# Eight gate tiles ahead of attention by four seven-product units, four plain units inside it

## The reference: a macaron layer with a gated mixer in its middle

```python
proj = u @ w_in                      # u is (1024, 1024), w_in is (1024, 4096)
# columns: xp 512 | q 512 | k 512 | v 512 | gate_logits 2048
y_pool = causal_pool_mixer(xp, pool_w_group, pool_scale) @ w_branch_pool
o_sb = stick_breaking_attention(q, k, v)      # 8 heads of 64, 128 query rows at a time
y_sb = o_sb @ w_branch_attn
g = sigmoid(gate_logits)
g_pool, g_sb = split(g, 2)                    # 8 tiles of 128 channels each
h = h + (g_pool * y_pool + g_sb * y_sb) @ w_out
```

## Time and profile before

| | |
|---|---|
| median of 3 runs | 1911.35 us (1911.08 to 1912.22) |
| the profiled execution | 1911.22 us, its span 1909.3 us |
| PE busy | 1899.8 us, 100% of the span, 8998 matmuls |
| DVE, ACT, POOL busy | 1370.5 us (72%), 799.4 us (42%), 135.0 us (7%) |
| granted PE clock | full in all 40 slices |
| DMA | 348.24 MB, 182 GB/s on average |

### The profile page before, as it was taken

One profiled execution on the slowest core, in us unless ns is written; L12 is line 12 of the kernel. 1 busy time (PEld: TensorE's weight loads), 2 busy tenths in 40 slices (PEclk: granted clock), 3 DMA queues, 4 the chain that ended last, 5 costly groups with the idle time before them and its releaser, 6 DMA issues.

```text
span 1909.3 us, 24938 instructions
## 1 busy us (share of the span) xinstructions
PE 1899.8 (100%) x8998; PEld 1591.0 (83%) x8998; DVE 1370.5 (72%) x1686; ACT 799.4 (42%) x1177; POOL 135.0 (7%) x157
## 2 busy tenths in 40 slices
PE   9999999999999999999999999999999999999998
PEld 9888888888888888888888888898888888888886
DVE  6977777784565786469677768889777777755655
ACT  7423232323434544324577762473323232334344
POOL 1000000000000200000145420010000000000001
PEclk9999999999999999999999999999999999999999
DMA  5456654558676733423866557634455445677665
GB/s 165 151 198 228 225 178 142 198 189 307 209 237 204 199 110 133 133 72 106 242 175 176 138 163 261 185 128 134 165 162 179 167 152 163 222 262 239 205 194 201
DMA packets 258419, 348.24 MB, mean 182 GB/s; under 512 B 29344, under 2 KB 161184, under 8 KB 255008
## 3 DMA queue, kind: packets, MB, share of 16 engines
q1 hardware_dynamic: 258016, 346.62, 56.2%
q10 hardware_dynamic: 320, 0.52, 0.1%
HBM read 233.83 MB, written 112.99 MB: 182 GB/s over the span
## 4 chain that ended last, share of the span: by engine, by line
PE 97%; DVE 1%; DMA 1%; ACT 0%; issue 0%; SPq 0%; POOL 0%; POOLq 0%; ACTq 0%
PE bank L1271 41%; PE bank L1327 8%; PE bank L1328 8%; PE bank L1329 8%; PE bank L1380 8%; PE bank L1520 7%; PE bank L1223 3%; PE bank L1430 2%; PE bank L1458 2%; PE bank L1488 2%; PE bank L1590 2%; PE bank L1609 1%; PE bank L1608 1%; PE bank L1198 1%; PE bank L1575 1%; PE bank L1573 1%
## 5 line engine op out<-in xcount | busy, mean ns | idle before, releaser
L2270 DVE TENSOR_TENSOR dn_lo<-dn_lo_raw,dn_hi 128x1024 fp32r<-128x1024 f32 x149 | 181.7, 1223 | 150.9 <-ACT dn_hi L1793 150.3
L1271 PE MATMUL bank<-hi_t,wa_lo 128*128 128x512 f32 x656 | 252.8, 389 | 0.0
L1271 PE MATMUL bank<-lo_t,wa_hi 128*128 128x512 f32 x656 | 252.8, 389 | 0.0
L1271 PE MATMUL bank<-hi_t,wa_hi 128*128 128x512 f32 x656 | 252.7, 389 | 0.0
L1793 ACT ACTIVATE dn_hi<-dn_lo_raw 128x1024 fp32r<-128x1024 f32 x149 | 157.9, 1061 | 220.2 <-DMA dn_lo_raw<-act_dram 220.2
L1327 PE MATMUL bank<-dn_hi 128*128 128x512 f32 x596 | 232.5, 390 | 0.0
L1329 PE MATMUL bank<-dn_lo,dn_hi 128*128 128x512 f32 x596 | 231.9, 389 | 0.0
L1328 PE MATMUL bank<-dn_hi,dn_lo 128*128 128x512 f32 x596 | 231.9, 389 | 0.0
L1271 PE MATMUL bank<-hi_b,wa_hi 128*128 128x512 f32 x492 | 190.4, 389 | 0.0
L1271 PE MATMUL bank<-lo_b,wa_hi 128*128 128x512 f32 x492 | 190.4, 389 | 0.0
L1271 PE MATMUL bank<-hi_b,wa_lo 128*128 128x512 f32 x492 | 190.4, 389 | 0.0
(11 more groups left out here) (275 smaller groups left out, 3846.0 us busy)
## 6 DMA issues: line engine op xcount, KB each, us to landing
wa_lo_raw<-in_ffn_w_gate_up_dram SPq DMA_DIRECT2D x87, 512.0 KB, 5.0
dn_lo_raw<-act_dram SPq DMA_DIRECT2D x149, 256.0 KB, 4.3
act_dram<-g SPq DMA_DIRECT2D x44, 512.0 KB, 4.4
wd_t<-in_ffn_w_down_dram SPq DMA_DIRECT2D x44, 512.0 KB, 6.7
act_dram<-s_of SPq DMA_DIRECT2D x88, 256.0 KB, 6.4
wd_dram<-wd_t SPq DMA_DIRECT2D x22, 1024.0 KB, 5.9
dn_lo_raw<-wd_dram SPq DMA_DIRECT2D x85, 256.0 KB, 3.3
dn_lo_raw<-in_ffn_w_down_dram SPq DMA_DIRECT2D x64, 256.0 KB, 3.0
```

The source lines that it names most:

```text
L1271: last = nc.tensor.matmul(acc, lhs, rhs, start=n == 0 and i != 2 and i < 5, stop=n == 11, skip_group_check=True)
L2270: return nc.vector.tensor_tensor(dst, raw, hi.bitcast(f32), ALU.subtract)
```

## The change

`EARLY` goes from 6 to 8. By the formulas this makes `MIX_UNITS` one gate unit longer (`NM` = 8: two of q and k, four of attention gates, two of `xp`), and `GATE_UNITS` one shorter (`NG` = 4: all eight kind 0 tiles in pairs, 16 banks, 384 matmuls). All eight attention gate tiles are then made by seven-product units. `U_C` falls from 13 to 12.

With eight units, the last of which must again end on the lower quad, unit 0 now takes the upper quad. So the second plain unit of q and k moves to banks 0 to 3, behind the first one, and waits for each bank to be emptied; the first seven-product unit waits for the last transpose instead of for banks, and the second one waits for the banks of the second plain unit. The ring buffers' places, counted from the end, turn by one. The rest of the diff restates parities: `b + NM + 1` becomes `b + 1`, `4 * m + b` becomes `b`, and the branch weights go to half `j % 2`.

```diff
-EARLY = 6
+EARLY = 8
 GATE_UNITS = tuple(((0, j), (0, j + 1)) for j in range(0, EARLY, 2)) + tuple(((0, j), (1, j)) for j in range(EARLY, KT))
...
                 for b in range(4):
                     th, ab = b // 2, b % 2
-                    if not fresh:
-                        pe.wait_ge(tr_free, 4 * NT)
+                    wait_bank(b, q)
...
-                        last = products(bank[:, b if fresh else 4 + b, :], par, ab, lambda kt: u_hi[:, kt, cols],
+                        last = products(bank[:, b, :], par, ab, lambda kt: u_hi[:, kt, cols],
...
             def mix_unit(b):
 
-                s = (b + NM + 1) % 2
+                s = (b + 1) % 2
                 for i in range(7):
                     place, hi, lo, (kind, slot) = PRODUCTS[i]
-                    if b < 2 and i in (0, 1, 3, 4):
-                        wait_bank(place, Q_A[b] + 1)
+                    if b == 0 and i == 0:
+                        pe.wait_ge(tr_free, 4 * NT)
+                    if b == 1 and i in (0, 1, 3, 4):
+                        wait_bank(place, Q_A[1] + 1)
...
             for j in range(KT):
-                branch_tile(j, (U_C + j) % 2, j // 2)
+                branch_tile(j, j % 2, j // 2)
...
-                nc.scalar.activation(ring_hi[n % 3][:, th * HALF:(th + 1) * HALF], bank[:, 4 * m + b, :], ACT.Copy,
+                nc.scalar.activation(ring_hi[n % 3][:, th * HALF:(th + 1) * HALF], bank[:, b, :], ACT.Copy,
...
-            act.wait_ge(raw_in[U_C % 2], 32 * (U_C // 2 + 1))
+            act.wait_ge(raw_in[KT % 2], 32 * (U_C // 2 + 1))
```

More of the change, by code:

```diff
@@ L1974, in mix_first @@
                 act.wait_ge(mb_prod, 7 * b + 1)
-                nc.scalar.activation(mix_dst(b, 0, 0), bank[:, 4 * ((b + NM + 1) % 2), :], ACT.Copy).then_inc(mb_copied, 1)
+                nc.scalar.activation(mix_dst(b, 0, 0), bank[:, 4 * ((b + 1) % 2), :], ACT.Copy).then_inc(mb_copied, 1)
             def mix_second(b):
@@ L1981, in mix_second @@
                     act.wait_ge(mb_add, 5 * b)
-                nc.scalar.activation(mid[:, :], bank[:, 4 * ((b + NM + 1) % 2), :], ACT.Copy).then_inc(mb_copied, 1)
+                nc.scalar.activation(mid[:, :], bank[:, 4 * ((b + 1) % 2), :], ACT.Copy).then_inc(mb_copied, 1)
             def mix_post(b, a, th, adds):
@@ L2238, in outputs_hi @@
                 nc.scalar.activation(o_piece(u_hi, i), o_piece(xu, i), ACT.Copy).then_inc(o_hi, 1)
-            act.wait_ge(raw_in[U_C % 2], 32 * (U_C // 2 + 1))
+            act.wait_ge(raw_in[KT % 2], 32 * (U_C // 2 + 1))
             act.wait_ge(gate_ready, GATE_LAST[NG - 2] + 1)
-            nc.scalar.activation(w_hi[:, U_C % 2, 0, 0:BR], w_raw[:, U_C % 2, 0, 0:BR], ACT.Copy).then_inc(whi, 1)
+            nc.scalar.activation(w_hi[:, KT % 2, 0, 0:BR], w_raw[:, KT % 2, 0, 0:BR], ACT.Copy).then_inc(whi, 1)
             for i in range(len(O_PARTS)):
@@ L2249, in split_branch @@
             def split_branch(j):
-                act.wait_ge(raw_in[(U_C + j) % 2], 32 * ((U_C + j) // 2 + 1))
+                act.wait_ge(raw_in[j % 2], 32 * ((U_C + j) // 2 + 1))
                 act.wait_ge(acc_ready, 4 * Q_C + 2 * (j - 1))
-                nc.scalar.activation(w_hi[:, (U_C + j) % 2, 0, 0:BR], w_raw[:, (U_C + j) % 2, 0, 0:BR], ACT.Copy).then_inc(whi, 1)
+                nc.scalar.activation(w_hi[:, j % 2, 0, 0:BR], w_raw[:, j % 2, 0, 0:BR], ACT.Copy).then_inc(whi, 1)
             for n in range(1, KT):
@@ L2719, in take_first @@
                 cols = slice(th * HALF, (th + 1) * HALF)
-                nc.vector.scalar_tensor_tensor(out=ring_lo[(2 * m + ab) % 3][:, cols], in0=bank[:, 4 * m + b, :], scalar=1.0 if ab else QSCALE,
+                nc.vector.scalar_tensor_tensor(out=ring_lo[(2 * m + ab) % 3][:, cols], in0=bank[:, b, :], scalar=1.0 if ab else QSCALE,
                                                in1=ring_hi[(2 * m + ab) % 3][:, cols].bitcast(f32), op0=ALU.mult,
@@ L2784, in mix_c11 @@
                 dst = mix_dst(b, 0, 0)
-                nc.vector.tensor_tensor(dst, bank[:, 4 * ((b + NM + 1) % 2) + 1, :], dst, ALU.add).then_inc(mb_add, 1)
+                nc.vector.tensor_tensor(dst, bank[:, 4 * ((b + 1) % 2) + 1, :], dst, ALU.add).then_inc(mb_add, 1)
             def mix_c22(b, part):
-                dst, s = mix_dst(b, 1, 1), (b + NM + 1) % 2
+                dst, s = mix_dst(b, 1, 1), (b + 1) % 2
                 if part:
@@ L2805, in mix_c12 @@
                 dve.wait_ge(mb_prod, 7 * b + 6)
-                nc.vector.tensor_tensor(mix_dst(b, 0, 1), bank[:, 4 * ((b + NM + 1) % 2) + 2, :], mid[:, :], ALU.add).then_inc(mb_add, 1)
+                nc.vector.tensor_tensor(mix_dst(b, 0, 1), bank[:, 4 * ((b + 1) % 2) + 2, :], mid[:, :], ALU.add).then_inc(mb_add, 1)
             def mix_c21(b):
                 dve.wait_ge(mb_prod, 7 * b + 7)
-                nc.vector.tensor_tensor(mix_dst(b, 1, 0), bank[:, 4 * ((b + NM + 1) % 2) + 3, :], mid[:, :], ALU.add).then_inc(mb_add, 1)
+                nc.vector.tensor_tensor(mix_dst(b, 1, 0), bank[:, 4 * ((b + 1) % 2) + 3, :], mid[:, :], ALU.add).then_inc(mb_add, 1)
             def mix_out(b, a, th, posts):
@@ L3145, in split_branch @@
                 dve.wait_ge(whi, U_C + j + 1)
-                dst, raw, hi = (flat(w[:, (U_C + j) % 2, 0, 0:BR]) for w in (w_lo, w_raw, w_hi))
+                dst, raw, hi = (flat(w[:, j % 2, 0, 0:BR]) for w in (w_lo, w_raw, w_hi))
                 nc.vector.tensor_tensor(dst, raw, hi.bitcast(f32), ALU.subtract).then_inc(wlo, 1)
```

4 lines of the change are left out of this document (2 added, 2 removed).

## The result

| | before | after |
|---|---|---|
| median | 1911.3 us (1911.08 to 1912.22) | 1921.45 us (1921.23 to 1923.36) |
| ratio, 95% interval | | 1.0055 (1.0044 to 1.0067) |
| profiled execution, span | 1911.2, 1909.3 us | 1922.66, 1920.7 us |
| PE matmuls | 8998 | 8986 |
| attention: first gate matmul to branch | 215.7 us | 208.6 us |

The prediction said 1912.8, range 1909.0 to 1916.0. The change is slower, and by twice as much as the worst case that I had priced, +4.7. The trace of after is of an execution 1.2 us above its median, so sums over the trace come out about 1 us above sums of medians.

A forecast was written before the change was run, and what follows sets the result against it. PE was taken to bound the kernel, busy 1899.8 of 1909.3 us. The terms +19.0 - 22.1 + 0.6 + 4.0 + 0.1 gave +1.6 us on 1911.22, so 1912.8 us, range 1909.0 to 1916.0.

The forecast's parts named there:

- the worst case that I had priced: Attention: the waits at the weighs at their upper bound of 7 us, making the change +4.7 us, 1915.9.
- Parts 1, 2, 3 and 5: Added seven-product unit +19.0 us; second plain unit in lower banks 0; 96 attention matmuls gone -22.1; end of attention +0.1.
- Part 4 (a): First logits of attention: PE arrives 0.7 us earlier and waits for the q load, +0.6 us, bounds 0 and 0.7.
- Part 4 (b) and (c): Waits at attention's weighs when fewer gate matmuls cover them: 4.0 us together, bounds 1.5 and 7.
- (c): Weighs, where DVE's scan or ACT's older work delays the answer: +1.0 us, fewer pieces and sigmoids counted against it.
- (b): The 32 weighs of odd steps: one or two fewer gate matmuls after the transposes, 3.0 us of added wait.
- Part 4 (d): Attention's other waits (transposes for scans, logits for sigmoids, transpose banks): slack suffices, none added on its own.
- The prediction's own sign: Length of attention: about 195 us expected; over 198 us would mean that the scan chain rules.
- The waits stay small: Rival: ACT and DVE follow PE closer, weigh waits 1.5 us or so, first logits 0.3; 1910.0 us, chance 0.25.
- The scan chain takes over: Rival: transposes, at_hi, at_lo, wide scan, at_lo, weigh over two steps set attention's pace; +4.7 us, 1915.9, chance 0.17.
- Its second reason: POOL's gate products starting just before wide scans delay them, 0.5 us in some six steps, 3 us inside the +4.7.

The follow-up runs named there:

- e11: The changed kernel itself, unchanged, run once more in a later batch; 1922.01 us.
- e2: The changed kernel with every weight piece moved to an odd step, the first piece of gate unit 1 to step 5; 1915.72 us.
- e3: The kernel before with 96 of attention's 480 gate matmuls left out, spread evenly, nothing else changed; 1901.06 us.
- e1: The changed kernel with the first piece of gate unit 1's weights placed at step 4 instead of 2; 1918.4 us.
- e4: The changed kernel with every DVE scan in attention cut to at most 512 columns; 1918.86 us.
- e12: The kernel before with 48 of attention's 480 gate matmuls left out, spread evenly; 1905.43 us.
- e9: The kernel of e2 with a further 96 gate matmuls of attention left out, 288 of 384 left; 1913.41 us.
- e6: The kernel of e2 with POOL's gate products cut from 512 to 8 columns; 1915.77 us.
- e13: The kernel of e2 with the scan cut to at most 512 columns; 1913.81 us.
- e7: The kernel of e2 with the transposes put ahead of the weigh in PE's odd steps; 1914.49 us.
- e16: The kernel before with every weight piece in an odd step; 1913.87 us.

## Why the prediction was wrong, by its own steps

*Parts 1, 2, 3 and 5 held.* +19.02 for +19.0; no gap in the first units; 96 matmuls went; behind attention nothing was lost (766.2 us, 766.8 before), and the branch's first matmul is 0.1 us late:

```profile
1154.45 0.47 PE L1457 MATMUL bank<-u_hi,w_hi 128*128 128x512 f32 x1
```

*Part 4 (a) held in kind*: 0.6 us was the sum, 0.9 the loss, over the bound of 0.7. In e11, the same kernel, it is 0.7, and the wait for q differs by more than that between executions.

*Part 4 (b) and (c), mis-sized: 4.0 for 9.2 us.* The gaps ahead of `weigh` grew by 7.5 us, past the upper bound of 7. The mechanism of the scan was right in place and nearly in size (0.23 us more on top of a slack of 0.1 us or less at seven tiles of type 2; 0.37 at five of them measured). What failed is the sentence in (c) that books the pieces as a credit, since there are fewer. Their number falls, but each of those left can still stand ahead of the very `at_lo` that an odd step needs, and with less cover it shows: 3.5 us of gaps at tiles 5, 7, 37 and 39, part of it the scan's, 2.7 by e2 on the clock. The sum by tile had only the slack of before, in which other pieces stood at other tiles. The other 1.7 us of the 9.2 lie behind the waits, not in them, and (b) priced nothing there: where a `weigh` has to wait for `at_lo`, its second matmul starts 0.22 us behind the first (982.56 to 982.79 above), where it is 0.11 otherwise. That is so in 22 of the 32 `weigh`s of after and in 6 of before, 1.8 us more.

*Part 4 (d), wrong: "none is added".* The largest single wait of all, 3.0 us, was added at the transposes of tile 1. With the 0.52 clock behind it, the stretch lost 4.9 us. (d) set the transposes against scans, sigmoids and banks, and gave the three banks 0.6 us of slack by the answer of ACT and DVE; it left out that ACT, ahead of the first `at_hi`, waits for the load of a weight piece, which doesn't come sooner when PE does. e3 shows it with the piece in its old place (a stop of 1.9 us). e1, which puts the piece behind `at_hi`, gives back 3.0 us. That the load landed 2.6 us later after the first logits than in before is on top of this, and why is open.

The prediction's own sign misled too: over 198 us of attention was to mean that the scan chain rules. The window took 205.3, and cutting the scan gave back only 2.6 us (e4).

*The rivals.* "The waits stay small" is out: 9.2 us were lost where it had 1.5. "The scan chain takes over" came nearest, as the point from which two steps of PE are shorter than the chain is passed (e3, e12, e9). But it too priced 7 us, the `weigh`s alone. Its second reason, 3 us for POOL's products, is not what happened. In after one scan is long in this way:

```profile
1089.45 2.37 DVE L3057 TENSOR_TENSOR_SCAN a<-keep,a 128x640 f32<-128x640 f32 x1
...
1089.19 1.28 POOL L3229 TENSOR_TENSOR gst<-gst,pool_y 128x512 f32<-128x512 f32 x1 [0.93 <-ACT gst L2218]
```

0.9 us more than such a scan takes otherwise (1.49, at 971.39), and two others by 0.26 and 0.54; PE didn't wait behind any, and e6 confirms it.

So of the 13.2 us that were lost, 3.0 (e1) and 2.7 (e2) can be had back by placing the pieces better, and 1.9 to 2.6 are the scan's (e13, e4). The rest, some 5 us, is by the rows the wait on the `at_hi`, `at_lo` way at the other types and for q; no variant got rid of it, it only changed places. What caused the loss is another sum: as e12 and e3 show in the kernel before, half of what is taken out is lost though nothing else is changed. 96 matmuls there are worth 10.4 us, and the front pays 19.0 for them, which makes 8.6 of the 10.1 us; the remaining 1.5 are for all that the change moved besides. None of the complete kernels beats before; e7, the best of those with the change, is 1.0017. Not tried was a list of piece steps fitted by hand against both DVE and POOL, or an earlier load of gate unit 1's weights.

## What to carry to other kernels

Where work of the bounding engine is moved out of a stage that it shares with a chain over slower engines, price the stage by a thinned run of the old kernel (leave the matmuls out), not by count times duration: here 96 matmuls were worth 10.4 us, not 22.1. What is placed by a formula from the same counts (here the weight pieces) moves with them; write the two placements side by side and read for each moved instruction what stands behind it in its queue. Ask also which loads keep their time when PE comes sooner. An engine at 75% busy tells nothing of the slack: the longest way from a result's release to its return does.

## What the runs showed of the hardware that was not expected

- Behind one stop of PE, 3.0 us, the granted clock was 0.52 for a slice, and 11 matmuls took 3.2 us; in e11 it was 0.63 from 962.4 to 965.6, behind the same stop. A stretch of the same work without that stop (e1) took 4.7 us less. Behind e3's stop of 1.9 us the clock stayed at 1.00.
- A scan of DVE that started 0.07 us behind a product on POOL took 2.31 us instead of 1.21. PE waited 0.86 us behind it, and 0.8 at a second such place: by the trace 1.7 of the 2.4 us that e16 is slower.
- Where `weigh` waits for `at_lo`, PE's second matmul starts 0.22 us behind the first, otherwise 0.11.
